# Hybrid encoder block on one core: each pair of modulation units moved to either side of the pair's first chunk, their sums between the halves of the second chunk

## The reference, cut to what matters

```python
c_act = jax.nn.silu(c)
mod = c_act @ w_ada[l] + b_ada[l]                  # (1, 6144): 24 units of 256 columns
shift1, scale1, gate1, shift2, scale2, gate2 = jnp.split(mod, 6, axis=-1)
h = modulate(rms_norm(x, norm1_w[l]), shift1, scale1)   # (1024 tokens, 1024 features)
...
proj = h @ w_in
q, k, v, xr, yr, g_attn, g_lru = jnp.split(proj, IN_SPLITS, axis=-1)
```

## Time and profile before

| | us |
|---|---|
| time, median of 3 runs | 2154.72 (2152.97 to 2156.53) |
| the profiled execution's own time | 2153.53 |
| its span | 2151.7 |
| TensorE busy | 2048.0 (95%) |
| VectorE busy | 1624.6 (76%) |
| ScalarE busy | 1261.2 (59%) |
| idle before `ps_headsums` L727, released by the DMA of `w_ada`, 28 to 72 us | 3.4 |
| idle before `ps_proj` L772, released by VectorE's `h_lo` L633, 28 to 72 us | 1.1 |

### The profile page before, as it was taken

How to read it: one execution, slowest core, us unless ns; L and a number is a source line. 1 busy time by engine, 2 the same in 40 slices (tenths; PEclk the granted TensorE clock), 3 DMA queues, 4 the chain that set the end, 5 groups by cost and what they waited for, 6 DMA issues and landing times.

```text
span 2151.7 us, 26217 instructions
## 1 busy us (share of the span) xinstructions
PE 2048.0 (95%) x10035; PEld 1688.4 (78%) x10035; DVE 1624.6 (76%) x1586; ACT 1261.2 (59%) x1173; POOL 143.8 (7%) x122
## 2 busy tenths in 40 slices
PE   6999989999999999895599999999999999999998
PEld 4777977888878888784488888888888888888886
DVE  5767656588865532556788899899998898888986
ACT  4422155477754322333377777777777777777774
POOL 3000000000000000002000000000000000000000
PEclk8999999999999999997799999999999999999999
DMA  8665120311012211236599999999999999999994
GB/s 282 182 185 160 40 60 2 84 44 45 25 51 93 82 49 59 70 118 225 187 371 383 385 384 381 392 384 384 381 389 387 383 382 383 391 384 389 383 380 160
DMA packets 245818, 511.01 MB, mean 237 GB/s; under 512 B 8012, under 2 KB 64760, under 8 KB 245752
## 3 DMA queue, kind: packets, MB, share of 16 engines
q1 hardware_dynamic: 236544, 484.32, 61.4%
q0 software_dynamic: 6608, 19.40, 3.6%
q10 hardware_dynamic: 2600, 6.38, 1.3%
HBM read 486.48 MB, written 16.78 MB: 234 GB/s over the span
## 4 chain that ended last, share of the span: by engine, by line
PE 51%; DMA 0%; DVE 0%; issue 0%; POOL 0%; ACT 0%; POOLq 0%
PE ps_gu L2291 32%; PE ps_down L2291 16%; PE ps_turn L2286 2%; DMA moe_x<-h_rows,slot_token 0%; POOL out_x L2271 0%; DVE moe_x_lo L2207 0%; ACT moe_x_hi L2173 0%; DVE moe_y L2230 0%; POOLq L2269 0%; POOLq L1729 0%
## 5 line engine op out<-in xcount | busy, mean ns | idle before, releaser
L2201 DVE TENSOR_TENSOR h_lo<-tiles,h_hi 128x2048 fp32r<-128x2048 f32 x252 | 566.0, 2288 | 70.5 <-ACT h_hi L2168 68.9
L2168 ACT ACTIVATE h_hi<-tiles 128x2048 fp32r<-128x2048 f32 x252 | 468.9, 1912 | 78.9 <-PE ps_down L2291 46.7
L2201 DVE TENSOR_TENSOR third_split<-tiles,third_split 128x2048 fp32r<-128x2048 f32 x128 | 287.5, 2287 | 41.3 <-ACT third_split L2168 40.3
L2168 ACT ACTIVATE third_split<-tiles 128x2048 fp32r<-128x2048 f32 x128 | 238.2, 1911 | 39.0 <-PE ps_down L2291 25.7
L2291 PE MATMUL ps_gu<-h_hi,moe_x_hi 128*128 128x512 f32 x640 | 250.6, 392 | 1.4 <-DVE moe_x_lo L2207 1.4
L2291 PE MATMUL ps_gu<-h_hi,moe_x_lo 128*128 128x512 f32 x640 | 249.3, 390 | 0.0
L2291 PE MATMUL ps_gu<-h_lo,moe_x_hi 128*128 128x512 f32 x640 | 248.9, 389 | 0.0
L2291 PE MATMUL ps_gu<-third_split,moe_x_hi 128*128 128x512 f32 x768 | 239.6, 393 | 0.0
L298 PE MATMUL ps_projected<-h_hi,hi_ring 128*128 128x512 f32 x496 | 193.9, 391 | 1.9 <-ACT tiles L1338 0.6
L298 PE MATMUL ps_projected<-h_hi,lo_ring 128*128 128x512 f32 x496 | 193.0, 389 | 0.0
L298 PE MATMUL ps_projected<-h_lo,hi_ring 128*128 128x512 f32 x496 | 193.0, 389 | 0.0
(11 more groups left out here) (360 smaller groups left out, 3768.3 us busy)
## 6 DMA issues: line engine op xcount, KB each, us to landing
tiles<-in_w_gate SPq DMA_DIRECT2D x64, 2048.0 KB, 10.1
tiles<-in_w_up SPq DMA_DIRECT2D x64, 2048.0 KB, 10.8
tiles<-in_w_down SPq DMA_DIRECT2D x64, 2048.0 KB, 11.0
tiles<-in_w_ada SPq DMA_DIRECT2D x24, 1024.0 KB, 8.4
tiles<-in_w_in SPq DMA_DIRECT2D x17, 1024.0 KB, 5.3
tiles<-in_w_in SPq DMA_DIRECT2D x16, 512.0 KB, 5.3
tiles<-in_w_lru_branch SPq DMA_DIRECT2D x8, 1024.0 KB, 5.1
v<-v ACTq DMA_DIRECT2D x48, 128.0 KB, 2.4
```

Of the source, the lines that this page charges most:

```text
L2168: nc.scalar.activation(half(w_hi(t), i), half(raw_tile(g, t), i), ACT.Copy).then_inc(hi_ready, 1)
L2201: nc.vector.tensor_tensor(half(w_lo(t), i), half(raw_tile(g, t), i), half(w_hi(t), i).bitcast(F32), ALU.subtract).then_inc(lo_ready, 1)
```

## The change

In each of the rounds 0 to 2 the second unit's rows are moved behind the first chunk, and the sums of the pair are moved into the second chunk, between its output column 0 and its output column 1. Before, a round was: rows, rows, chunk 2m (12 matmuls), sums, chunk 2m+1 (12 matmuls). After, it is: rows, chunk 2m (12), rows, chunk 2m+1 column 0 (6), sums, chunk 2m+1 column 1 (6). Round 3 has no units; its two chunks have the same order as before. No instruction is added or taken away, and no other engine's program is changed.

```diff
-            def first_two(c):
+            def first_two(c, columns=(0, 1)):
 
                 pe.wait_ge(h_lo, c + 1)
-                for i in range(2):
+                for i in columns:
                     k = item(i)
...
             for m in range(4):
                 if m < 3:
                     ada_rows(2 * m + 2)
+                first_two(2 * m)
+                if m < 3:
                     ada_rows(2 * m + 3)
-                first_two(2 * m)
+                first_two(2 * m + 1, (0,))
                 if m < 3:
                     ada_add(2 * m + 2)
                     ada_add(2 * m + 3)
-                first_two(2 * m + 1)
+                first_two(2 * m + 1, (1,))
```

## The result

The changed kernel takes 2160.79 us in the median of 7 runs (2159.13 to 2163.6), the kernel before 2154.29 (2152.97 to 2156.53, 7 runs): ratio 1.003, 95% interval 1.0021 to 1.004, 6.5 us slower. The profiled execution took 2160.41, its span is 2158.6, 6.9 us above before's.

The account below looks back on a forecast made before the run. TensorE was taken to bound the stage, with the modulation chain hidden before the change. The terms 0.1 - 0.3 + 1.8 + 2.5 gave +4.1 us on 2154.7, so 2158.8 us; range 2155.9 to 2162.2.

Parts of the forecast that it names:

- The start: Round 0 up to the sums of units 2 and 3: fetch wait gone, sums at 42.7 against 42.61, +0.1 us.
- The chain: From a pair's sums to the next pair's first chunk: 5.32 us before chunk 2, 4.87 before chunks 4 and 6.
- The steps: TensorE's stretches to the first sums, then chunks 2, 4 and 6: +0.1, -0.3, +1.8 and +2.5 us.
- The covered moves: First stage: the second unit's copy (0.42 us) lies beside six matmuls (1.49), and later fetches have slack; no cost.
- wait of 1.72 us at 230.40: TensorE wait in the profile before, after which the clock stayed at 1.00; taken as harmless.
- rival 1: Clock falls at the wait before chunk 6, slowing chunks 6 and 7: +5.8 us, 2160.5; chance 0.28.
- Everything behind it shifts alike: Behind chunk 6, expected to start near 68.4: all later work starts later by the same sum, +4.1 us.
- rival 4: First stage: chain stays hidden and the change gains, -1.3 us, or -3.0 with an early clock rise; chance 0.04.
- rival 2: Clock rises early behind chunk 0 and does not fall: +3.2 us, 2157.9; chance 0.13.
- The rule of the Trainium skill: Loop whose every round waits and starts at the low clock; by it all three new waits would cost, 1.7 us each.

Follow-up runs that it names:

- sums-only run: Kernel before with only the sums moved between the halves of the second chunk, both units' rows still ahead of the first chunk: 2159.62 us, ratio 1.0027.
- rows-only run: Kernel before with the second unit's rows moved behind the first chunk, sums directly behind them, ahead of the whole second chunk: 2155.72 us, ratio 1.0008.
- filled waits: Changed kernel with spare TensorE work in its three new waits and two waits of the value projection: 2157.9 us, ratio 1.0019 to the kernel before.
- busy delays: Kernel before with 24, 39, 46 or 69 spare matmuls ahead of chunk 6: 2158.48, 2160.9, 2161.35 and 2164.12 us.
- run that was 3.6 us early: Kernel before with unit 3's rows moved inside chunk 0 in round 0 only, plus spare transposes in waits to hold the clock: 2155.09 us, ratio 1.0003.

## Why the prediction was right, and where it was short

- *The start.* The fetch wait is gone, and chunk 0 starts at 34.63 (34.91 predicted). The sums came at 42.40 (42.7). The idle time ahead of chunk 0 was 2.13, not 1.3, because the rows of unit 2 still ran at the full clock there (1.07 us at 31.43, where they took 1.93 at 31.71 in before); in the changed kernel's second profile they took 1.93, and the idle time was 1.30.
- *The chain.* 5.29, 4.86 and 4.85 us, against 5.32, 4.87 and 4.87. The late start of VectorE on chunk 2 came again (1.82 us of wait). The new waits were 1.85, 1.41 and 2.40 (2.1, 1.7 and 2.6 predicted), each 0.2 to 0.3 shorter, since the work beside the chain took 3.4 us and not 3.2 (what made it longer was not tested).
- *The steps.* -0.2, -0.3, +1.9 (58.00 - 47.69 = 10.31 against 8.44) and +2.6, together +3.95, against 0.1 - 0.3 + 1.8 + 2.5 = 4.1. Both parts of the change were seen rightly: the sums-only run has the three waits, the rows-only run loses 0.6 us at chunk 6.
- *The covered moves.* The copy of unit 3 ended at 41.46, ahead of the sums; no fetch ended a wait in rounds 1 to 3.
- *What was short.* The time is 6.5 us longer, not 4.1. The term that was mis-sized is the clock. I priced it as a rival at one place, 1.7 us at the last wait, and took the wait of 1.72 us at 230.40 as harmless because the clock had stayed up there. In the changed kernel the clock fell at that same wait in one execution, and behind waits of 1.85 and 2.41 us in another. One row of one execution was no ground for calling a wait harmless. The filled waits put the size at 3.0 us. That the measured time lies in the range, and close to rival 1 (2160.5), is partly luck: rival 1 put a fall at the wait ahead of chunk 6, and the profile that lies 6.9 us above before's has none there; the other profile has one, and one more behind the wait ahead of chunk 2.
- "Everything behind it shifts alike" was wrong as well. The busy delays show that 1.7 to 6.9 us of lateness behind chunk 5 cost more by the end, 3.2 to 3.9 us by the medians, though no spare wait was put in.
- In rival 4 the second value takes 1.7 us for an early rise of the clock where rival 2 takes 0.9; with 0.9 it is -2.2 and not -3.0. Nothing in the forecast hangs on it.

The rule of the Trainium skill that I weighed ("TensorE: Matmul & The Clock Gate", section "HAM oscillation — how this bites in real kernels") described the kind of loss. In that section's loop, though, TensorE waits some 3 to 5 us for a transfer in every round, longer than any of these waits, so it was no ground for saying that all three would cost. The traces agree that work behind a wait may start at the low clock, but not at every wait of every execution, and it happened behind waits of 1.49 to 2.42 us.

*Open.* Why the kernel before shows no fall of the clock between 45 and 280 us in two profiles, while it has the same two waits in the value projection. The run that was 3.6 us early lost its gain as well, so it is not lateness alone. Nor do the delays show a regular dependence on their length. What decides whether the clock falls at a given wait stays open.

## What to carry to other kernels

Before work is put between a producer and the long chain that hangs on it, measure the chain from its first instruction to its consumer and count what is left beside it: here 4.9 us against 3.4, and the three waits that came of it took 5.7 us together, for one fetch wait of 2.6 us and a chain wait of 1.06. If only the first round has the wait, change only the first round; here that took the wait away, but a gain in the whole time is not shown. Short waits of TensorE cost more than their length where the clock falls behind them; spare matmuls in such a wait are a cheap test of that share. One profile in which the clock stays up at a wait does not clear that wait.

## What the hardware showed beyond the expected

- The clock fell to half for 3.4 us behind waits of 1.49 (217 us), 1.72 (236 us), 1.85 (47 us) and 2.41 us (68 us), and behind the same waits it stayed at 1.00 in the other profile of the same kernel. In the sums-only run it fell behind one of 2.42 us (66 us).
- One such stretch at the value projection made a profile 1.4 to 1.5 us later, two of them 2.8 to 3.0.
- A delay of 1.7 us of pure TensorE work made the kernel 4.9 us slower (2.8 to 7.1), one of 6.9 us 10.5 us (6.7 to 12.7).
- Spare work of 1.2 to 1.8 us (as the timeline lists it) in each of five waits, which computes nothing, made the changed kernel 3.0 us faster by the medians.
